# Final folds of a second state scan in quarters of the groups instead of halves, with each pair of output matmuls behind its own quarter

## What is computed

```python
# pooling: four channel groups, windows 2, 4, 8, 16
pm = _pool_mean_1d(ug, w) if rows is None else _pool_mean_2d(ug, w, rows)
outs.append(jnp.einsum("blc,cd->bld", pm - ug, pool_w[gi].astype(F32)))
...
# state space: 32 groups of 16 channels, 64 complex states each, two directions
_, h = lax.associative_scan(_combine, (jnp.broadcast_to(a_bar, bu.shape), bu), reverse=rev, axis=1)
y = y + jnp.real(jnp.einsum("gpn,blgn->blgp", cmat, h))
...
y = jax.nn.gelu(y.reshape(bsz, n, D_SSM))
out = y * jax.nn.sigmoid(jnp.dot(y, p["ssm_w_glu"].astype(F32)))
```

## Time and profile before

| | |
|---|---|
| median of 3 runs | 1285.36 us (1285.09 to 1287.89) |
| the profiled execution's own time | 1285.23 us |
| its span in the trace | 1283.1 us |
| PE busy | 1210.6 us (94%) |
| DVE busy | 853.9 us (67%) |
| ACT busy | 331.2 us (26%) |
| POOL busy | 445.3 us (35%) |

### The profile page before, as it was taken

How to read it: one execution, slowest core, us unless ns; L and a number is a source line. 1 busy time by engine, 2 the same in 40 slices (tenths; PEclk the granted TensorE clock), 3 DMA queues, 4 the chain that set the end, 5 groups by cost and what they waited for, 6 DMA issues and landing times.

```text
span 1283.1 us, 18548 instructions
## 1 busy us (share of the span) xinstructions
PE 1210.6 (94%) x6479; PEld 1052.2 (82%) x6479; DVE 853.9 (67%) x1349; ACT 331.2 (26%) x615; POOL 445.3 (35%) x376
## 2 busy tenths in 40 slices
PE   3879998995899999999999999999999999999997
PEld 0179997664687888889899899899899899898996
DVE  2988999999886587464564664664654655645648
ACT  2374333222423475012011011011021120120114
POOL 1100000321100441642743734725626526527430
PEclk9979999996999999999999999999999999999999
DMA  7913333875711232120120110110210201201004
GB/s 181 328 35 101 106 115 100 257 183 124 225 35 43 89 99 82 34 66 33 33 65 16 49 54 19 58 49 16 65 35 31 65 33 33 65 33 33 33 1 147
DMA packets 79372, 101.66 MB, mean 79 GB/s; under 512 B 25763, under 2 KB 61767, under 8 KB 79077
## 3 DMA queue, kind: packets, MB, share of 16 engines
q1 hardware_dynamic: 56848, 80.00, 20.3%
q0 software_dynamic: 5200, 17.67, 4.5%
q10 hardware_dynamic: 17284, 3.47, 1.3%
HBM read 89.53 MB, written 9.49 MB: 77 GB/s over the span
## 4 chain that ended last, share of the span: by engine, by line
PE 87%; DVE 4%; issue 3%; DMA 2%; ACT 2%; ACTq 2%; DVEq 0%
PE bank L1376 25%; PE bank L1378 25%; PE bank L1377 25%; DMA raw<-in_w_ada 2%; PE bank L1389 2%; PE bank L1569 1%; PE bank L1568 1%; PE bank L1508 1%; PE bank L1481 1%; ACTq L527 1%; PE bank L1589 1%; PE bank L1567 1%; PE bank L1422 1%; DVE acc L1360 1%; DVE x_lo L982 1%
## 5 line engine op out<-in xcount | busy, mean ns | idle before, releaser
L513 POOL TENSOR_TENSOR acc<-acc,gated 128x512 f32<-128x512 f32 x270 | 373.2, 1382 | 375.7 <-DVE gated L1312 339.2
L1376 PE MATMUL bank<-x_hi,w_hi 128*128 128x384 f32 x960 | 324.0, 338 | 4.2 <-issue 2.7
L1378 PE MATMUL bank<-x_hi,w_lo 128*128 128x384 f32 x960 | 321.7, 335 | 0.0
L1377 PE MATMUL bank<-x_lo,w_hi 128*128 128x384 f32 x960 | 321.5, 335 | 0.0
L1312 DVE TENSOR_TENSOR gated<-bank,gate_b 128x512 f32<-128x512 f32 x270 | 182.2, 687 | 113.5 <-PE bank L1378 85.5
L1376 PE MATMUL bank<-w_hi,f_hi 128*128 128x512 f32 x576 | 224.2, 389 | 1.2 <-DVE w_lo L1293 1.2
L1378 PE MATMUL bank<-w_hi,f_lo 128*128 128x512 f32 x576 | 224.4, 390 | 0.0
L1377 PE MATMUL bank<-w_lo,f_hi 128*128 128x512 f32 x576 | 224.3, 389 | 0.0
L849 ACT ACTIVATE relu<-bank 128x384 f32<-128x384 f32 x96 | 47.2, 493 | 649.3 <-PE bank L1378 646.3
L1302 DVE TENSOR_TENSOR f_tmp<-relu 128x384 f32<-128x384 f32 x96 | 65.9, 686 | 204.4 <-ACT relu L849 204.4
L1376 PEld LDWEIGHTS bank<-x_hi,w_hi 128*128 128x128 f32 x960 | 180.7, 188 | 7.8 <-issue 6.2
(11 more groups left out here) (310 smaller groups left out, 1427.8 us busy)
## 6 DMA issues: line engine op xcount, KB each, us to landing
raw<-in_w_mlp SPq DMA_DIRECT2D x64, 512.0 KB
raw<-in_w_ada SPq DMA_DIRECT2D x48, 512.0 KB
x_tile<-in_x_sample POOLq DMA_DIRECT2D x8, 512.0 KB, 7.8
raw<-in_w_in SPq DMA_DIRECT2D x8, 512.0 KB
raw<-in_w_out SPq DMA_DIRECT2D x8, 512.0 KB
x_again<-in_x_sample POOLq DMA_DIRECT2D x8, 512.0 KB, 3.9
out<-acc SPq DMA_DIRECT2D x8, 512.0 KB, 2.6
u_rows<-proj ACTq DMA_DIRECT2D x4, 576.0 KB, 3.3
```

Of the source, the lines that this page charges most:

```text
L513: GP.tensor_tensor(a, a, BT[i % 4][:], ALU.add).then_inc(s.acc, 1)
L1376: mm(out, sh_, mh, start=first, stop=False)
L1377: mm(out, sh_, ml, start=False, stop=False)
L1378: return mm(out, sl, mh, start=False, stop=last)
```

## The change

The last level of the scan is cut into folds over 4 groups instead of 8 for block 1; block 0 keeps its two halves. A block-1 fold then has 288 elements a partition, there are eight folds of five instructions instead of four, and block 1 adds eight to `filled` instead of four. The order is quarter by quarter, forward then backward. PE's wait follows: pair `i` of block 1 waits for quarter `i // 2`. The thresholds of block 0 stay as they were.

```diff
@@ -1138,10 +1138,11 @@
             up(2, 0, G, slice(0, 9, 8), slice(4, 13, 8))
             for d in range(2):
                 up(1, d * GB, GB, slice(0, 13, 4), slice(2, 15, 4))
-            for h in range(2):
+            nq = 4 if b else 8
+            for h in range(GB // nq):
                 for d in range(2):
-                    q0 = d * GB + 8 * h
-                    ins = fold(b, 0, q0, 8, hb[:, q0:q0 + 8, 0:15:2, :], hb[:, q0:q0 + 8, 1:16:2, :])
+                    q0 = d * GB + nq * h
+                    ins = fold(b, 0, q0, nq, hb[:, q0:q0 + nq, 0:15:2, :], hb[:, q0:q0 + nq, 1:16:2, :])
                     ins.then_inc(s.filled, 1)
                     dve.wait_ge(s.filled, 4 * b + 2 * h + d + 1)
                     between(step[0])
@@ -1556,7 +1557,7 @@
         def y_pair(b, i):
             if i == 0:
                 pe.wait_ge(loc_in[b], 16 * 2 * L)
-            pe.wait_ge(s.filled, 4 * b + 2 * (i // 4) + 2)
+            pe.wait_ge(s.filled, 4 + 2 * (i // 2) + 2 if b else 2 * (i // 4) + 2)
             if b or i >= 4:
                 pe.wait_ge(s.y_ev, 8 * b + i - 3)
             else:
```

## The result

The changed kernel took **1290.47 us** (median of 7 runs, 1289.8 to 1291.46); the kernel before took 1286.25 in 7 runs (1285.02 to 1288.15), and the ratio is 1.0031, 95% interval 1.0022 to 1.0040. It is slower, by 2.8 to 5.1 us of 1286. Measured once more beside the later experiments, the ratio was 1.0026 (1.0015 to 1.0036). The forecast was 1288.7, in a range from 1286.9 to 1291.0.

What follows compares the result with a forecast made beforehand. PE waits for DVE's folds, and DVE's second window stands only 0.91 us ahead of map 3. The GLU comes 3.3 us later: 1285.23 + 3.3 = 1288.5 profiled, median 0.13 above, 1288.7 us; range 1286.9 to 1291.0.

Steps and rivals of the forecast that it cites:

- The folds: DVE, last folds of block 1: eight new folds at 2.45 us each take 19.60, 3.81 us more on DVE.
- Rival C: DVE folds: short folds are cheaper than the 288-element row; 1284.5 with no fixed part, 1286.7 with half; 13%.
- y: PE's eight pairs: start 3.00 us earlier, without waiting for quarters; y ends 3.0 us earlier, gaining the GLU nothing.
- The maps: PE, pooling maps: map 3 waits for the second window, 2.97 us later, plus 0.34; GLU 3.3 us later.
- The restart: PE at map 3: its first matmul behind a pause takes 0.82 instead of 0.48, so 0.34 us more.
- rival D: ACT's `y_hi(1)`: y rows, not the second window, decide the GLU; the whole 3.0 us come through, 1282.4; 6%.
- The clock: PE, maps 3 to 5: a pause of nearly 5 us lowers the clock to 0.50; maps don't slow, cost nothing.
- Rival B: PE, maps 3 to 5: they slow with the clock like local matmuls, 1.4 to 2.8 us more, 1290.1 to 1291.5; 18%.
- rival A: The forecast itself: whole kernel at 1288.0 to 1289.4 us; 63%.

Runs made afterwards that it cites:

- Experiment 1: Changed kernel with its eight quarter folds, but PE's pairs of block 1 wait for halves again; 1289.12 us, 1.0023 of the kernel before.
- Experiments 2: Changed kernel with the low parts of the GLU and first output weight tiles moved later on DVE, GLU's behind both pooling windows; 1287.99 us, ratio 1.0015 to before.
- kernel 4: Kernel before, no quarters, with the GLU weight tiles moved behind the pooling windows on DVE and output tiles later; 1286.08 us, ratio 0.9996 to before.
- 5: Changed kernel with only block 1's first half in quarters, second half in two 8-group folds, and weight tiles moved behind on DVE; 1284.94 us, ratio 0.9990 to before.
- kernel 8: kernel 4 (no quarters) with ACT's rounding of the first y rows ahead of the evictions of maps 3 to 5; 1285.59 us, ratio 0.9993 to before.
- kernel 7: Kernel 5 with ACT's rounding of the first y rows ahead of the evictions of maps 3 to 5; 1282.81 us, ratio 0.9965 to before.

## Why the prediction held

**The folds.** 3.81 us more on DVE were forecast from the row of another shape with 288 elements; 19.59 - 15.79 = 3.80 came. Each of the 40 instructions took 0.45 or 0.46 us. Rival C, cheaper short folds, is gone. The 360 ns by the cycle table of the Trainium skill (VectorE: DVE Perf Modes, "The TRN2 errata") didn't come here either: 0.45 us is the least of the 40.

**y.** The first pair came 3.01 us earlier (forecast 3.00) and no pair waited. y ended 3.44 us earlier after the first fold (26.45 against 29.89) and not 3.0, as the pairs ran at the lower clock for 3.2 us at their start instead of 6.2; this went into the pause before map 0, 1.55 us where 1 was forecast. `pad(1)` held up evictions 4 to 6 to 322.8, 1.2 us after the forecast 321.6 in an execution that stands 1.37 later, and the last eviction came when its pair was done. The path of the y rows got the 3 us and spent them in front of ACT. Experiment 1 is the proof: taking the early start away again cost the stage nothing.

**The maps.** Forecast for the GLU was 3.3 us later, measured 3.37. How it is made up differs from the working: map 3's record starts 3.21 us later (33.97 to 37.18) and maps 3 to 5 take 0.15 longer, where 2.97 and 0.34 were set down. Both terms were read from the chain, in which a piece starts where the one before it ends. The timeline of PE before has the records themselves, which overlap:

```profile
309.37 0.66 PE L1567 MATMUL bank<-u_chunks,local_b 128*128 128x144 f32 x2
...
330.69 2.94 PE L1589 MATMUL bank<-pool_in,pool_w_sb 128*128 128x384 f32 x4
333.45 1.10 PE L1591 MATMUL bank<-pool_in,pool_w_sb 128*128 128x256 f32 x2
334.37 0.64 PE L1592 MATMUL bank<-pool_in,pool_w_sb 128*128 128x128 f32 x2
```

Map 3 started at 330.69 and not at 330.87, 0.73 us behind the window and not 0.91; so a start at 333.84 is 3.15 later. The restart costs 0.82 - 0.66 = 0.16, not 0.34. The two slips are the same 0.18 us and cancel, so the sum was right although its terms weren't. Experiments 2 and 4 show that the window decides in the changed kernel and PE in the kernel before, which excludes rival D, the y rows; so does experiment 1, where y came 4.9 us later and the GLU didn't.

**The clock.** It fell around the new pause, as forecast, and maps 3 to 5 ran at the lower level without slowing, as the turned state matmuls do. The table of stretches of the changed kernel, PE alone (stretch, length, PE busy and instructions, granted clock, DMA), for these maps and for the first GLU matmuls:

```profile
335.27:339.70 4.43, 4.43 (x8) 0.50 1.04 243
343.20:347.10 3.90, 3.90 (x12) 0.50 0.30 78
```

From map 3's start to the end of map 5's last record it is 4.47 us at 0.50 and was 4.32 at 1.00 before (33.97 to 38.29). Rival B, with its 1.4 to 2.8 us, is out. The doubling in the Trainium skill (TensorE: Matmul & The Clock Gate, "Back-to-back issue gap") holds for the GLU's matmuls nearly, 0.32 against 0.17 us, and not for these maps: the 256 columns of the third map took 0.92 us (339.10 - 338.18) at 0.50 and 0.92 (334.37 - 333.45) at 1.00.

**The whole.** The forecast was right in its sign and its mechanism, and 1.8 us low in the time. The 1290.47 lies above the span of rival A, the forecast (1288.0 to 1289.4), and in that of B (1290.1 to 1291.5), whose mechanism did not come; the second median, 1289.66, lies between the two. That the first measurement fell into the range is thus owed to the part of it that was put there for B, and that part is luck. Of the 1.8 us, 0.9 is the base: the median of before, 1285.36 from three runs, is 1286.25 from seven. The two profiled executions stand 5.24 us apart: 3.37 in the stage, 1.37 ahead of it, and 0.3 for 12 GLU matmuls at the lower level where 10 had run there before; 0.2 stays unassigned. The same account closes for all eleven profiled executions: the time less the start of the last folds, less the stage, less 0.15 us for each GLU matmul at the lower level, is 945.3 to 945.5 us, whatever the kernel. The start (296.64 to 299.10) and the matmuls at the lower level (none to 18) move an execution by up to 2.5 and 2.7 us, nearly as much as the change costs. That the change by itself costs more than the stage shows is not borne out: the second measurement, 1.0026, is 3.3 us.

## What to carry to other kernels

Cutting an instruction in two brings its first half forward and makes its second half late by the part of the cost that has no size (here 0.19 us of 0.79), and everything behind it on that engine is late with it. Before cutting, follow both: who wants the first half, and what stands behind the last one; here the consumer's gain ended in a wait for the same engine, whose lead over the consumer had been less than 1 us. The early start was worth something only where the weight tiles stood behind the windows on DVE and no more than the first half was cut: 0.93 us of the stage between kernels 4 and 5, and 0.73 between 8 and 7, with ACT's move in both. The larger part of kernel 7's gain is that of the two moves, which need no cut.

## What the runs showed of the hardware beside this

**Matmuls that the clock does not slow.** In one y pair the local matmul went from 0.48 to 0.26 us when the clock rose and the turned one stayed at 0.49 to 0.51; a map took 3.6 ns a column at either level (0.92 us for 256). Both read float32 columns that lie 8 or 9 elements apart; whether the distance makes it was not tried by itself.

**The clock after like pauses.** Ten of the eleven profiles have a pause of PE of 1.9 to 3.4 us ahead of the GLU and 10 to 18 GLU matmuls at the lower level behind it; at 0.15 us each that is more than 1 us between executions of kernels with the same stage (10 in the kernel before, 18 in kernel 4). In kernel 7's profile no GLU matmul ran at the lower level: its pause was 2.06 us, the maps before it ran at 1.00, and the GLU did as well. Kernel 8's pause of 2.31 us, behind maps without a pause, was followed by 15 at the lower level. The tables of stretches, the start of the GLU of kernel 7 and that of kernel 8:

```profile
336.00:340.00 4.00, 3.94 (x23) 1.00 0.96 288
```

```profile
339.20:342.00 2.80, 2.75 (x9) 0.50 0.99 257
```

Fifteen matmuls at 0.15 us are 2.2 us. The two profiled executions stand 1286.78 - 1281.36 = 5.42 us apart: 2.46 ahead of the first fold, where the two kernels do the same, 0.73 in the stage and 2.2 behind it. They are the fastest of 7's runs and the slowest of 8's, and no others were traced, so how the 2.8 us between the medians divide is not shown. All five runs of kernel 7 (up to 1283.36) lie under all eleven of kernel 8 (from 1283.70), so it is not one lucky execution, but what pause the clock bears in general stays open.

The same goes on in the y pairs: in 7 and 8 they were at the lower level for a shorter time and y ended 0.4 us earlier than in 5 and 4 (28.33 and 28.74, 29.45 and 29.87 after the first fold). In 8, where the rows decide, the stage is shorter by that: with y at 29.87 its GLU would come at some 40.6 (an estimate from these two figures and the 40.15), near the 40.5 expected, and the quarters would be worth 1.1 to 1.2 us. In 7 the stage gains little by it, as the rounding was done 0.52 us before DVE came to its rows.
